# The mLSTM stage moved ahead of the rotary stage, with another share of the woven-in attention in each

## What is computed

```python
mstate, ha = run_chunks(mlstm_chunk, mstate, (qa, ka, va, ig, lf))        # A: mLSTM
ha = head_rms(ha.transpose(0, 2, 1, 3), g_head_a) * jax.nn.sigmoid(ao.astype(f32))
gstate, hb = run_chunks(gla_chunk, gstate, (qb, kb, vb, la))              # B: gated linear attention
qc, kc, vc = rope(heads(cq, H_C), pos), rope(heads(ck, H_C), pos), heads(cv, H_C)
hc = window_fn(qc, kc, vc).reshape(B, T, -1)                              # C: dilated window attention
hd = sb_fn(qd, kd, vd, b_sb).reshape(B, T, -1)                            # D: stick-breaking attention
mixed = jnp.concatenate([ha.astype(h.dtype), hb.astype(h.dtype), hc, hd], -1)
```

## Time and profile before

| | |
|---|---|
| time, median of 3 runs | 3015.59 us (3015.39 to 3025.89) |
| profiled execution: its own time, and its span | 3005.96 us, 3003.8 us |
| PE busy | 2572.5 us (86%) |
| DVE busy | 1052.2 us (35%) |
| ACT busy | 855.4 us (28%) |
| mean granted clock of TensorE | 0.888 of full |
| 605.90 to 829.95 us: rotary and mLSTM stages of the first layer | 224.05 us |

### The profile page before, as it was taken

The page is one execution under the profiler, slowest core; times in us unless marked ns, Lnnn a source line. Parts: engine busy times, 40 slices in busy tenths (PEclk is TensorE's granted clock), DMA queues, the critical chain, the costliest instruction groups (busy, mean ns, idle before and its releaser), DMA issues. The chain is left out here.

```text
span 3003.8 us, 41766 instructions
## 1 busy us (share of the span) xinstructions
PE 2572.5 (86%) x16304; PEld 2113.3 (70%) x16304; DVE 1052.2 (35%) x1636; ACT 855.4 (28%) x1455; POOL 62.2 (2%) x68
## 2 busy tenths in 40 slices
PE   5999889959777867999969998899587878679998
PEld 5998687735544546998769986877354555469986
DVE  3332332233454424332243323221434644243322
ACT  3221222122423423222232213111223244232212
POOL 0000000011100000000000000000111000000000
PEclk9999989967787768999979998899787877789999
DMA  3332132144555232222132322221445552223321
GB/s 110 84 91 78 56 103 71 42 133 128 141 155 168 83 109 63 78 78 89 43 85 79 90 84 68 84 73 40 147 133 147 163 149 84 95 78 84 91 75 55
DMA packets 316199, 285.91 MB, mean 95 GB/s; under 512 B 38360, under 2 KB 281216, under 8 KB 316048
## 3 DMA queue, kind: packets, MB, share of 16 engines
q1 hardware_dynamic: 306832, 250.33, 28.2%
q0 software_dynamic: 9216, 33.56, 3.5%
HBM read 270.24 MB, written 13.58 MB: 94 GB/s over the span
## 5 line engine op out<-in xcount | busy, mean ns | idle before, releaser
L206 PE MATMUL ps<-f_h_hi,f_w_hi 128*128 128x288 f32 x2048 | 609.4, 298 | 15.8 <-DVE f_h_lo L293 15.8
L207 PE MATMUL ps<-f_h_lo,f_w_hi 128*128 128x288 f32 x2048 | 608.4, 297 | 0.0
L208 PE MATMUL ps<-f_h_hi,f_w_lo 128*128 128x288 f32 x2048 | 608.2, 297 | 0.0
L206 PEld LDWEIGHTS ps<-f_h_hi,f_w_hi 128*128 128x128 f32 x2048 | 389.9, 190 | 16.5 <-DVE f_h_lo L293 16.5
L207 PEld LDWEIGHTS ps<-f_h_lo,f_w_hi 128*128 128x128 f32 x2048 | 390.0, 190 | 0.0
L208 PEld LDWEIGHTS ps<-f_h_hi,f_w_lo 128*128 128x128 f32 x2048 | 389.5, 190 | 0.0
L239 DVE TENSOR_TENSOR f_w_lo<-f_room,f_w_hi 128x2048 fp32r<-128x2048 f32 x96 | 220.1, 2293 | 324.2 <-ACT f_w_hi L233 324.2
L206 PE MATMUL ps<-f_w_hi,f_a_hi 128*128 128x512 f32 (+1 forms) x640 | 253.9, 397 | 8.7 <-DVE f_a_lo L545 8.7
L207 PE MATMUL ps<-f_w_lo,f_a_hi 128*128 128x512 f32 (+1 forms) x640 | 252.8, 395 | 0.0
L233 ACT ACTIVATE f_w_hi<-f_room 128x2048 fp32r<-128x2048 f32 x96 | 182.8, 1904 | 245.0 <-PE ps L208 245.0
L208 PE MATMUL ps<-f_w_hi,f_a_lo 128*128 128x512 f32 (+1 forms) x640 | 251.3, 393 | 0.0
(11 more groups left out here) (316 smaller groups left out, 3607.7 us busy)
## 6 DMA issues: line engine op xcount, KB each, us to landing
f_room<-in_w_ffn_in SPq DMA_DIRECT2D x128, 512.0 KB, 5.3
f_room<-in_w_ffn_out SPq DMA_DIRECT2D x64, 512.0 KB, 4.2
sa_vn<-in_cache_sb_v SPq DMA_DIRECT2D x256, 128.0 KB
pr_w_raw<-in_w_in SPq DMA_DIRECT2D x60, 512.0 KB, 4.5
sa_kn<-in_cache_win_k SPq DMA_DIRECT2D x96, 128.0 KB, 2.6
sa_vn<-in_cache_win_v SPq DMA_DIRECT2D x96, 128.0 KB
sa_kn<-in_cache_win_k SPq DMA_DIRECT2D x16, 512.0 KB, 4.1
sa_vn<-in_cache_win_v SPq DMA_DIRECT2D x16, 512.0 KB
```

The source lines that it names most:

```text
L206: pe.matmul(out, stat_hi, mov_hi, start=start, stop=False, skip_group_check=True)
L207: pe.matmul(out, stat_hi, mov_lo, start=False, stop=False, skip_group_check=True)
L208: return pe.matmul(out, stat_lo, mov_hi, start=False, stop=stop, skip_group_check=True)
```

## The change

The two stages change places, the ticks are dealt out anew, and one small part of the sample attention comes later.

```diff
-PACE = (3, 27, 40)
+PACE = (25, 28, 40)
...
-MASK_TICK, QUERY_TICK = 6, 20
+MASK_TICK, QUERY_TICK = 6, 30
...
-            rotary(nc, E, M, l, O, C, side, paced(0, PACE[0], [1] * 4))
-            mlstm(nc, E, M, l, I, O, C, side, paced(PACE[0], PACE[1], ML_STEPS))
+            mlstm(nc, E, M, l, I, O, C, side, paced(0, PACE[0], ML_STEPS))
+            rotary(nc, E, M, l, O, C, side, paced(PACE[0], PACE[1], [1] * 4))
             gla(nc, E, M, l, I, O, C, side, paced(PACE[1], PACE[2], GLA_STEPS))
```

## The result

The changed kernel took 3027.89 us (median of 20 runs, 3017.54 to 3036.46), the kernel before 3015.28 us in the same comparison (20 runs, 2991.94 to 3030.48). The ratio is 1.0041, with a 95% interval from 1.0022 to 1.0061: 12.6 us slower, with 6.6 to 18.4 us inside the interval. The forecast was 3039.6 us and 24 us slower. So the sign was right, and the size about half. The profiled execution of the changed kernel has a span of 3030.8 us, 27.0 us more than that of before, so the two single executions differ by twice as much as the medians.

The account below looks back on a forecast made before the run. The prediction took different parts to be bound by SyncE's queue, VectorE chains, TensorE, then chains again. Its terms summed to +12.0 us a layer, +24.0 over two, on the 3015.59 us median: 3039.6 us, range 3014 to 3055.

Parts of the forecast that it names:

- (a): Start to mLSTM's step 3: 58.4 us before, 35.1 after, three ticks fewer done; -23.3 us a layer.
- (b): mLSTM's step 3 to first score unit: VectorE's chain starts behind two ticks, not one; +3.5 us a layer.
- (c): mLSTM's score units and states: 14 ticks instead of 13, TensorE the bound; +3.3 us a layer.
- (d): Last state matmul to head's transposes: VectorE the bound, a weighing ahead of the division waits for ScalarE; +1.2 us a layer.
- (e): Head's transposes to next stage: ScalarE's stick operations of tick 24 come last; +1.2 us a layer.
- (f): Rotary stage by itself behind mLSTM, with ticks 25 and 26 alone under it; +25.5 us a layer.
- (g): GLA: drops tick 35 (2.0 us), a weighing (2.7) comes sooner, plus four query operations; +0.6 us a layer.
- the chains are hidden: Rival: TensorE's clock and surrounding ticks absorb chains in mLSTM; 4 us a layer, 3023.6 us; chance 0.26.
- TensorE never runs dry: Rival: rotary products finish before tick 25 is used up, fewer gaps keep full clock; 2999.6 us; chance 0.09.
- the floor of 17.6: Least rotary stage length: three ticks at full clock 7.7, transposes 6.6, end 3.3 us.
- The rival of the falling clock: Longer stretches without matmuls leave TensorE at 1.2 GHz for more units; +6.2 us a layer, 3052 us; chance 0.11.
- rotary's lost cover: Rotary's load wait and products, formerly covered, become exposed; with other losses exceeds 8.4 us freed at mLSTM's start.

Follow-up runs that it names:

- experiment 1: Changed kernel with tick 0's six constants and bias issued on SyncE ahead of its sixteen value loads: 3014.51 us, ratio 1.0014 to the kernel before.
- experiment 2: Kernel before (old order) with tick 0's constants and bias issued ahead of its value loads: 2998.22 us, ratio 0.9935.
- experiment 12: New order without rotary stage, ticks 25 to 27 behind mLSTM's last transposes, tick 0's constants and bias ahead of mLSTM's seven constants: 2982.47 us, ratio 0.9904.
- experiment 3: Changed kernel with shares (24, 27, 40), so mLSTM holds 24 ticks as before the change: 3032.25 us, ratio 1.0066 to the kernel before.
- experiment 4: Kernel before (old order) with one tick more in mLSTM, one less in GLA, and four query operations later: 3031.82 us, ratio 1.0063.
- experiment 5: Changed kernel with the two rotary tables loaded in the mLSTM stage: 3024.68 us, ratio 1.0045 to the kernel before.
- experiment 6: Changed kernel with rotary tables loaded in mLSTM and rotary products behind score units 10 to 14: 3016.16 us, ratio 1.0026 to the kernel before.

## Why the prediction was right in sign and too large

*What bounds the kernel, and (a).* Right: SyncE's queue sets TensorE's start. Experiments 1, 2 and 12 move it by moving loads alone. The term was 1.7 us too small a gain, most of it in tick 0's start: I added 3.7 us to the 18.1 of before, and 1.9 and 1.0 came. The issue did move as I had it (626.76 - 608.15 = 18.6 us in; before, the bias went out 14.7 us in), but before, TensorE started 3.5 us after that issue, and now 1.4.

*(b), (c).* Right in mechanism. The tick among the units costs 4.1 us at an equal clock and not 3.3; the chain ahead of the units 2.7 to 2.8 and not 3.5. The forecast had mLSTM near 210 us, and it took 203.0 and 206.1: of the first layer's 7 us, 5.6 are units that ran at 0.83, where the 109.7 it started from ran at 0.77.

*(d).* The bound on VectorE was right; the size was 2.5 and not 1.2. VectorE ends L884 at 796.9, and tick 23's L2140 still stands ahead of L913 on TensorE until 798.0, which my sum didn't have. Experiment 3 gives 2.2 us back and experiment 4 pays 2.7 and 1.9 in the old order: they hang on the deal of the ticks and not on the order.

*(e).* Right to 0.1 us.

*(f).* This is the term that was mis-sized most, 1.4 and 3.4 us. I took the transposes, 6.6 us, from the old rotary stage, whose clock was 0.59. They took 5.2 us in the first layer and 4.0 in the second. TensorE in the kernel before, and in the two layers of the changed one:

```profile
633.58 0.47 PE L832 MATMUL ps<-ident,x 128*128 128x128 f32 x1 [1.25 <-ACT TR L816]
...
824.16 0.42 PE L834 MATMUL ps<-ident,x 128*128 128x128 f32 x1
...
2329.66 0.27 PE L834 MATMUL ps<-ident,x 128*128 128x128 f32 x1
```

In the first layer a transpose still took 0.42 us, as in the old stage; what fell away is the wait of 1.25 us for ScalarE's copy. In the second layer, where the stage had a clock of 0.87, it took 0.27. The wait for `ro_sin`, and VectorE's chain behind it, were as forecast; experiments 5 and 6 show them worth 2 to 4 and 1 us a layer.

*(g).* Near zero, as the forecast had it, but not by the two effects that I added (-2.0 and +2.7, which give +0.7 even without the query operations, not +0.6): with one tick fewer the old order's GLA gained nothing, and three more cost 15 us. A tick's price there is not TensorE's time for it.

*The rivals.* That the chains are hidden is out: (b), (d), (e) all show. That TensorE never runs dry is out: it waits 6.02, 1.98 and 2.36 us in the rotary stage; and with the products hidden the stage still takes 19.0 us. In the second layer of experiment 6 ticks 25 and 26 alone took 8.1 us, where the floor of 17.6 had 7.7 for three, tick 27 took 2.6, the transposes 4.0 and not 6.6, and loads and barrier 3.7 with the wait for TensorE ahead of them. The rival of the falling clock is not supported: the changed kernel's clock in its units is 0.83 and 0.79, that of before 0.77 and 0.83.

*The attribution.* The prediction put the loss on rotary's lost cover. Experiment 4 shows a loss of the same size from one tick more in mLSTM at the old order, and experiment 3 the same loss from the new order with the old share. So the two edits don't add: by the ratios either costs 19 or 20 us (10 at the least), both together 12.6 (18.4 at the most). That the pair costs less than either alone is not shown, as the intervals overlap. The forecast has some luck in it too: its errors cancel in part. A layer, (c) and (d) were too low by 0.8 and 1.3 us, (a), (b), (f) and (g) too high by 1.7, 0.7, 2.4 and 0.8, which leaves 3.5. In the new order the 25th tick moves the stick operations of tick 24 out of the rotary stage, where they cost 4 us, to the end of mLSTM, where they cost 1.2. Why experiment 3's units were slow at nearly the same clock stays open.

## What to carry to other kernels

When a stage is moved for the sake of the waits at its start, first list what stands ahead of the awaited load on the issuing queue: here moving sixteen loads behind seven small ones gave 20 us in the old order, where the reordering cost 12.6. Joining the two stages as well took 2.4 and 6.8 us a layer outside the units, which the times can't tell from nothing. Price a woven-in piece of work by what it costs in each stage when one more is put in, not by its matmuls: 4.1 us or more among the score units, some 2 in a head chain by its place, 5 in GLA, and nothing back when GLA lost one. And compare stages only at equal granted clock: an untouched stage differed by 9 us between two executions, most of a small change's effect.

## What the runs showed of the hardware

The clock of a single execution moves an untouched stage. In the kernel of experiment 1 the prompt attention of layer 2 had its slowest pass, against 148.75 us at 0.75 before:

```profile
2423.31:2590.11 166.80, 142.32 (x854) 90.19 (x854) 66.85 (x154) 67.24 (x160) 0.00 (x0) 0.65 0.30 93
```

A small bias load that was issued early in its stage took longer until TensorE could start (first layer):

| bias issued | TensorE starts | after the issue | kernel |
|---|---|---|---|
| 18.6 us in | 20.0 | 1.4 | changed |
| 14.7 | 18.1 | 3.5 | before |
| 9.0 | 13.7 | 4.7 | experiment 1 |
| 3.9 | 9.6 | 5.6 | experiment 12 |
| 3.8 | 8.9 | 5.0 | experiment 2 |

In experiment 12 the second layer had 4.4 us for the same issue. In each of these kernels GpSimd issues four gathers in the first 6 us of the stage, beside the constants. So an earlier issue returned only part of what it moved. Which transfer delays the load was not tested.

And a stage whose last DMA is a gather on GpSimd ended well behind it. In the old order's rotary stage the gather ended at 640.99 us and the last operation of any engine, on ScalarE, at 641.5, and the next stage began at 645.41: 4.4 us after the gather. In the second layer it was 4.4 us again (2138.23 and 2142.68). Where SyncE's value loads came last, the next stage began 1.1 us after them (experiment 6).
